# Weaving the first quarter of the output product into the last RWKV chain

## The reference, cut to what matters

```python
ya_l = chunk_gmlp(...)                  # 512 columns  = 4 tiles of 128
yb_l = rwkv_mixer(...)                  # 768 columns  = 6 tiles
yc_l = na_mixer(...)                    # 768 columns  = 6 tiles
mix_l = matmul(concatenate([ya_l, yb_l, yc_l]), w_out)       # (512 x 2048) @ (2048 x 2048)
xl = layer_norm(ALPHA * xl + g1 * mix_l, ln1_g, ln1_b)
xl = layer_norm(ALPHA * xl + g2 * sq_relu_mlp(xl * (1 + sc2) + sh2, w_up, w_down), ln2_g, ln2_b)
```

## Time and profile before

| | us |
|---|---|
| median of three runs | 3344.65 (3338.05 to 3346.8) |
| the profiled execution, its own time | 3334.03 |
| its span, first to last instruction | 3332.2 |
| mean granted clock | 0.959 of full speed |
| last small matmuls of pair 5 ahead of its chain end | 1625.3 |
| first matmul of the output product | 1687.9 |
| last matmul of the output product | 1863.6 |

### The profile page before, as it was taken

The page is one execution under the profiler, slowest core; times in us unless marked ns, Lnnn a source line. Parts: engine busy times, 40 slices in busy tenths (PEclk is TensorE's granted clock), DMA queues, the critical chain, the costliest instruction groups (busy, mean ns, idle before and its releaser), DMA issues.

```text
span 3332.2 us, 70508 instructions
## 1 busy us (share of the span) xinstructions
PE 3097.9 (93%) x30308; PEld 2582.9 (78%) x30308; DVE 1578.5 (47%) x1999; ACT 745.7 (22%) x1103; POOL 1057.0 (32%) x482
## 2 busy tenths in 40 slices
PE   6799997999995999999879899999999999999996
PEld 0677875787774999999768688888888888888885
DVE  0777768347865444555422644343333333333335
ACT  0322222012222222222122321212121222222221
POOL 0343333444330000000034344444444444444442
PEclk7799998999997999999889999999999999999998
DMA  9665657222423111110142122222222222222222
GB/s 406 232 221 199 211 197 246 79 71 105 153 87 151 50 45 51 53 53 14 42 189 100 63 96 94 100 91 98 94 94 94 94 94 94 94 96 97 96 96 107
DMA packets 97666, 387.40 MB, mean 116 GB/s; under 512 B 10912, under 2 KB 12704, under 8 KB 90912
## 3 DMA queue, kind: packets, MB, share of 16 engines
q1 hardware_dynamic: 72096, 289.45, 23.9%
q10 hardware_dynamic: 25056, 92.42, 7.8%
q0 software_dynamic: 288, 2.10, 0.2%
HBM read 352.73 MB, written 31.20 MB: 115 GB/s over the span
## 4 chain that ended last, share of the span: by engine, by line
PE 64%; DVE 3%; DMA 1%; issue 1%; ACT 0%; SPq 0%; POOL 0%; ACTq 0%; DVEq 0%; POOLq 0%
PE bank L884 16%; PE bank L885 16%; PE bank L886 16%; PE bank L632 12%; PE bank L648 1%; PE bank L708 1%; DMA buf<-small_lncol 1%; PE bank L696 1%; PE bank L776 0%; PE bank L774 0%; DVE buf L1781 0%; DVE buf L1782 0%; PE bank L656 0%; DVE buf L1492 0%; DVE buf L1737 0%
## 5 line engine op out<-in xcount | busy, mean ns | idle before, releaser
L498 POOL TENSOR_TENSOR buf<-buf 128x1024 fp32r<-128x1024 f32 x288 | 696.9, 2420 | 1610.4 <-ACT buf L1264 1610.4
L884 PE MATMUL bank<-buf 128*128 128x512 f32 x2304 | 903.6, 392 | 19.1 <-DVE buf L1702 18.5
L885 PE MATMUL bank<-buf 128*128 128x512 f32 x2304 | 903.2, 392 | 0.0
L886 PE MATMUL bank<-buf 128*128 128x512 f32 x2304 | 903.0, 392 | 0.0
L1264 ACT CAST buf<-buf 128x1024 fp32r<-128x1024 f32 x288 | 302.5, 1050 | 1252.9 <-PE bank L886 1251.9
L884 PEld LDWEIGHTS bank<-buf 128*128 128x128 f32 x2304 | 432.6, 188 | 117.4 <-issue 20.3
L886 PEld LDWEIGHTS bank<-buf 128*128 128x128 f32 x2304 | 432.6, 188 | 97.2
L885 PEld LDWEIGHTS bank<-buf 128*128 128x128 f32 x2304 | 432.6, 188 | 96.7
L632 PE MATMUL bank<-buf 64*64 64x64 f32 x13248 | 427.4, 220 | 22.8 <-issue 10.6
L522 PE MATMUL bank<-buf 128*128 128x512 f32 (+1 forms) x1168 | 430.1, 368 | 17.8 <-POOL buf L492 11.8
L632 PEld LDWEIGHTS bank<-buf 64*64 64x64 f32 x13248 | 411.6, 136 | 34.2 <-issue 30.2
(11 more groups left out here) (215 smaller groups left out, 2426.0 us busy)
## 6 DMA issues: line engine op xcount, KB each, us to landing
buf<-stream SPq DMA_DIRECT2D x382, 512.0 KB, 3.2
buf<-adarows ACTq DMA_DIRECT2D x108, 512.0 KB, 4.9
buf<-ada SPq DMA_DIRECT2D x32, 1024.0 KB, 12.9
scaled_keys<-buf ACTq DMA_DIRECT2D x18, 768.0 KB, 5.6
buf<-scaled_keys SPq DMA_DIRECT2D x18, 768.0 KB, 6.9
buf<-adarows SPq DMA_DIRECT2D x20, 512.0 KB, 6.3
buf<-tokens SPq DMA_DIRECT2D x4, 1536.0 KB, 21.9
buf<-bias ACTq DMA_DIRECT2D x6, 1024.0 KB, 5.2
```

The costliest lines, as they stand in the source:

```text
L498: G.tensor_tensor(wl2[b % SPLIT2], raw2[b], wh2[b % SPLIT2].bitcast(F32), ALU.subtract).then_inc(split2, 1)
L884: pe.matmul(bank[:, :], lh, rh, start=start, stop=False)
L885: pe.matmul(bank[:, :], lh, rl, start=False, stop=False)
L886: return pe.matmul(bank[:, :], ll, rh, start=False, stop=stop)
```

## The change

**Mixer tiles are split where they are made.** `gated` now multiplies in place, then casts into `late_h` and subtracts into `late_l`, both resident, so the RWKV tiles are no longer stored. Attention makes `mst` (high) and `mlow` (low), gMLP overwrites its buffers with high and low parts; both are stored as two DRAM tensors and loaded back as `early_h`, `early_l` (2 x 2.5 MB) during pair 5, ahead of the wait for its last products. The rows of the output weight are permuted on the host so that the ten early tiles come first.

**The product is woven in.** `mixer_product` is a generator of 32 groups of six matmuls per column block. Block n = 0 is advanced one group after each of the ten chain steps, two after `read`, four after `mean`, the rest after `variance`. Pieces 5, 6, 7 wait for `R["done"]` of 2, 4, 6. `normed(4)` moves behind chain step 1 and `gated(4)` behind step 3. ACT makes the high parts of pieces 0 to 7 inside `act_core`.

**Gate rows go through DRAM.** After gMLP, ACT stores the two gate columns to `gate_rows` element by element; they are read back as broadcasts. The 32 DVE copies, 32 PE products and 8 ACT copies go.

**Layout.** Buffers of the core and the second half are placed anew, so that pieces, early tiles and tokens can land while the core still runs.

```diff
+        def mixer_product(pe, n):
+            for c in range(KT // 2):
+                pos = 8 * n + c
+                pe.wait_ge(split2, pos + 1)
+                if n == 0 and c == 0:
+                    pe.wait_ge(mix_ld[0], 16)
+                    pe.wait_ge(mix_ld[1], 16)
+                if n == 0 and c >= 5:
+                    pe.wait_ge(R["done"], 2 * (c - 5) + 2)
+                for m in range(4):
+                    if c == 0 and n >= 2:
+                        pe.wait_ge(E["oev"], 4 * n + m + 1)
+                    for k in range(2):
+                        mm = triple(pe, banks[4 * (n % 2) + m], ...)
...
+                    yield
...
# pe_core
+            ready(pe, ("rc", BPAIRS - 1, 0), ("rc", BPAIRS - 1, 1))
+            groups = mixer_product(pe, 0)
             for n in range(1, NC - 1):
                 chain(BPAIRS - 1, n)
+                advance(groups, 1)
             read(BPAIRS - 1)
+            advance(groups, 2)
             mean(BPAIRS - 1)
+            advance(groups, 4)
             variance(BPAIRS - 1)
+            finish(groups)
...
# act_core, behind pair 5
+            for pos in range(4):
+                act_high_part(once, pos, 32, 0)
             read(BPAIRS - 1)
+            act_high_part(once, 4, 32, 0)
             square(BPAIRS - 1)
             deviation(BPAIRS - 1)
-            store(BPAIRS - 1)
+            for pos in range(5, 8):
+                act_high_part(once, pos, 32, 0)
...
# dve_core, gated
-                dve.wait_ge(mst_out, 16 * (1 + CPAIRS + j))
-                V.tensor_tensor(mst, yc, late[j % 2][:, SEQ:], ALU.mult).then_inc(R["done"], 1)
+                step(V.tensor_tensor(yc, yc, late[j % 2][:, SEQ:], ALU.mult))
+                step(V.tensor_copy(late_h[:, j, :], yc))
+                V.tensor_tensor(late_l[:, j, :], yc, late_h[:, j, :].bitcast(F32), ALU.subtract).then_inc(R["done"], 1)
...
             for n in range(1, NC - 1):
                 chain(BPAIRS - 1, n)
+                if n == 1:
+                    normed(BPAIRS - 2)
+                if n == 3:
+                    gated(BPAIRS - 2)
...
# SP
+            ready(sp, ("rc", last - 1, 1), ("gv", last, 2))
+            sp.dma_start(raw2[0], stream2[0]).then_inc(rawld2[0], 16)
...
+            sp.dma_start(early_h.bitcast(F32), mixhd.rearrange("k p t -> p k t")).then_inc(mix_ld[0], 16)
+            sp.dma_start(early_l.bitcast(F32), mixld.rearrange("k p t -> p k t")).then_inc(mix_ld[1], 16)
+            ready(sp, ("z", last, 2), ("w", last, 2))
+            for b in range(1, RING2):
                 sp.dma_start(raw2[b], stream2[b]).then_inc(rawld2[b], 16)
+            ready(sp, ("rc", last, 0), ("rc", last, 1), ("y", last - 1))
+            sp.wait_ge(R["done"], last)
+            sp.wait_ge(gates_out, 32)
             sp.dma_start(xr, xtok).then_inc(E["x"], 16)
+            sp.dma_start(grow1, gates[0:1].rearrange("o k p -> o (k p)").to_broadcast([P, D])).then_inc(E["grow"], 16)
...
# act_gmlp; act_second_half issues lncol, grow2, lng, lnb once R["done"] is 6
+            act.wait_ge(mod_ev, 6)
+            for c in range(2):
+                act.dma_start(gates[c].rearrange("k p -> p k"), modv[:, 2 + 3 * c, :, 0], allow_slow_non_contiguous=True).then_inc(gates_out, 16)
...
# dve_gmlp, per tile j (before: add, multiply)
+                V.tensor_tensor(gout[j], gout[j], gu[j], ALU.mult).then_inc(A["vch"], 1)
+                V.tensor_copy(gouth[j], gout[j]).then_inc(A["vch"], 1)
+                V.tensor_tensor(goutl[j], gout[j], gouth[j].bitcast(F32), ALU.subtract).then_inc(A["done"], 1)
```

More of the change, by code:

```diff
@@ L298, in build_block @@
         eye = masks[:, P * (4 + 2 * len(LEVELS)):]
[L299 to L308, removed]
+        fc(192)
+        AH, BH, KH = fc(NI * T), fc(NI * T), fc(NI * T)
+        BT, KTT, GT, cV, RH = [fc(NI * T)], [fc(NI * T)], fc(NI * T), fc(TOK), [fc(NL * T)]
+        fc(256)
+        VT, late, RB, RK = [fc(TOK)], [fc(2 * SEQ)], [fc(NL * T)], [fc(NL * T)]
+        BT.append(fc(NI * T))
+        KTT.append(fc(NI * T))
+        W = fc(NI * T)
+        RH.append(fc(NL * T))
+        AT, GV, TT, XT, X, LT = (fc(NI * T) for _ in range(6))
         VT.append(fc(TOK))
-        RH.append(fc(NL * T))
-        Z, W, TR, NK, M = (fc(NI * T) for _ in range(5))
         RB.append(fc(NL * T))
@@ L331, in build_block @@
         lncol, hscl, hshf = f2(2 * KT), f2(KT), f2(KT)
[L332 to L336, removed]
+        dtmp = [f2(512) for _ in range(2)]
+        hTl = f2(KT * SEQ, F32R).rearrange("p (k t) -> p k t", k=KT)
+        hidl = f2(FT * SEQ, F32R).rearrange("p (k t) -> p k t", k=FT)
         second.close()
@@ L354, in build_block @@
         xmod, xhigh, xsplit = sem("tokens_modulated"), sem("tokens_high_part"), sem("tokens_split")
-        mixraw_ld = [sem(f"mixer_outputs_loaded_{q}") for q in range(4)]
+        mix_ld = [sem(f"mixer_{part}_parts_loaded") for part in ("high", "low")]
+        gates_out = sem("gate_rows_stored")
         z_ev = sem("projections_copied")
@@ L888, in pe_second_half @@
         def pe_second_half(pe):
[L890 to L904, removed]
-                        t.wait(split2, 16, pos + 1)
-                        if n == 0:
-                            pe.wait_ge(E["mixl"], 2 * c + 2)
-                        for m in range(4):
-                            if c == 0:
-                                t.wait(E["oev"], 8, 4 * n + m + 1)
-                            for k in range(2):
-                                mm = triple(pe, banks[4 * n + m], mixh[:, 2 * c + k, P * m:P * m + P],
-                                            mixl[:, 2 * c + k, P * m:P * m + P], wh2[pos % 2][:, 512 * k:512 * k + 512],
-                                            wl2[pos % 2][:, 512 * k:512 * k + 512], c == 0 and k == 0, c == 7 and k == 1)
-                            if c == 7 and m < 3:
-                                mm.then_inc(E["omm"], 1)
-                        mm.then_inc(used2, 1)
+            for n in range(1, 4):
+                finish(mixer_product(pe, n))
             for k in range(KT):
@@ L1101, in act_projections, with act_high_part @@
                     squares(j + 1)
+        def act_high_part(t, pos, per, base):
+            t.wait(rawld2[pos % RING2], 16 * per // RING2, 16 * ((base + pos) // RING2) + 16)
+            if base + pos >= SPLIT2:
+                t.wait(used2, per, base + pos + 1 - SPLIT2)
+            nc.scalar.copy(wh2[pos % SPLIT2], raw2[pos % RING2]).then_inc(high2, 1)
         def act_core(act):
@@ L1635, in dve_attention @@
             w("pv", 8)
[L1636 to L1639 removed]
+            t.wait(mst_out, 32, 32)
+            rows = lambda a: a.rearrange("p (r b c) -> p b r c", b=4, c=QC)
+            outs = Q[4][:, :].rearrange("p (b r c) -> p b r c", b=4, c=QC)
+            t.step(V.tensor_copy(rows(mst), outs))
+            V.tensor_tensor(rows(mlow), outs, rows(mst.bitcast(F32)), ALU.subtract).then_inc(C["done"], 1)
             assert t.n == t.per, ("c", t.n)
@@ L1895 @@
     up, down = tiles(a["w_up"][0]), a["w_down"][0]
-    parts = [wide_tiles(a["w_out"][0])]
+    mixer = list(range(APAIRS)) + list(range(APAIRS + BPAIRS, KT)) + list(range(APAIRS, APAIRS + BPAIRS))
+    parts = [wide_tiles(a["w_out"][0].reshape(KT, P, D)[mixer].reshape(D, D))]
     for e in range(EFF):
```

141 lines of the change are left out of this document (64 added, 77 removed).

## The result

| | before | after |
|---|---|---|
| median of 4 runs, us | 3345.02 (3338.05 to 3346.8) | 3314.16 (3310.14 to 3319.46) |
| profiled execution, us | 3334.03 | 3313.88 |
| its span, us | 3332.2 | 3312.1 |

The ratio is 0.9921 with the 95% interval 0.9905 to 0.9938: 26 us faster by the ratio, 31 by the two medians, where 45 were forecast. Applied to 3344.65 the ratio gives 3318.2, which is just beyond the upper end of the range, 3318.

The account below looks back on a forecast made before the run. PE was taken as the bound, busy 93%, with 62.6 us between pair 5's small matmuls and the output product to fill. Gain 47.3 less 2.2 for earlier additions gave 45.1: 3299.5 us against the runs' median, range 3287 to 3318.

Parts of the forecast that it names:

- PE in the chain and the product: From pair 5's last small matmul to the output product's end: 1625.3 to 1816.6; gain 47.3 us.
- The narrow place, piece 4: Reload into piece 4's buffer during the weave: landed at 1651, needed by ACT at 1654; if late, some 5 us.
- The last mixer tile: After the variance at 1661.8, tile done at 1669.8; piece 7 wants it at 1678, 8 us of cover.
- The two stalls at steps 3 and 5: In the woven chain PE waits for DVE behind normed(4) and gated(4): 1.7 and 2.15 us, together 3.9.
- changes of shape: PE switches 22 times between 64 x 64 and 128 x 128 matmuls in the weave: 0.1 us each, 2.2 together.
- rival B: Weave too thin: stalls lower the clock or piece 4 comes late; gain 25 to 38, time 3307 to 3320; chance 0.22.
- sign that the prediction listed as wrong: PE waiting for POOL's low parts or last DVE subtraction, clock near 0.7, late ACT copies, or longer attention turns.
- Blocks 1 to 3 and all behind them run as before, shifted.: Output product after block 0, and everything later including the MLP: same duration as before, only earlier; no cost set.
- the early loads in pair 5 cost nothing: Loading early mixer tiles during pair 5: no term for slowing PE was set.
- What is added earlier: Extra work before the weave costs 2.2 us: gMLP 1.4, attention 0.75; core's longer gated and the gate store covered.
- The element-wise gate store: After gMLP, two stores of 2048 four-byte runs take ACT 10.6 us to issue, covered by idle time: cost 0.
- the prediction's slow case: Gate store decides from 0.25 us per run; at 0.31 PE waits 62 us, time 3361; chance 0.03.

Follow-up runs that it names:

- Runs 4 to 6: In order: changed kernel, small tiles moved behind MLP low parts, 3283.14 us; same move in kernel before, 3321.48; first one's operands shifted 8 to 320 words, 3282.29 to 3319.58.
- run 8: Changed kernel without the cast and subtraction that make low parts of the ten gMLP and attention tiles: 3309.83 us, ratio 0.9909.
- the kernel with the burst: Kernel before plus two useless DRAM-to-DRAM copies of 2.5 MB each at the time of the early loads: 3345.95 us, ratio 1.0025.

## Why the prediction fell short

**Right, by its own steps.** PE in the chain and the product: from the last small matmul of pair 5 to the product's end 190.8 us, by the prediction 191.3 (1625.3 to 1816.6). The 0.84 us ahead of the chain, which the view puts down to issue, stand where the prediction had 0.75 of waiting for the `rc` copies. Clock 1.00 through the read, 5.82 us for its 192 matmuls, 5.8 forecast. `lncol` is gone from the chain. The narrow place, piece 4, held: PE did not wait for POOL anywhere in the chain and the product. The last mixer tile: variance 1680.5, its last subtraction at 1691.06 on DVE, so done 11.2 us after the variance where 8.0 were forecast: 3.2 late against 8 us of cover. One of its operations, the cast, took 2.59 us and not 0.44, and ended right behind a subtraction of POOL (1688.35 to 1690.75): one blocking, of the kind that the prediction priced at up to 2.39, here on an operation with a single input. The Trainium skill (SBUF — State Buffer, Who interferes with whom) names casts among those that can take the shared port pair, and this row agrees.

**Right in sum only.** The two stalls at steps 3 and 5 are 0.67 and 0.94 us, not 1.7 and 2.15. A chain step without a stall is 1.96 us, from 1655.72 to 1657.68 in the timeline above, where the matmuls alone were set to 1.6. The 0.36 between them hold two changes of shape, so each costs about 0.18 where 0.1 was taken, 22 of them 4.0 us (an estimate: it puts the whole difference down to the changes). The two errors, 2.2 us too much and 1.8 too little, cancel, which is luck.

Luck too is where the time landed. 3314 us, or 3318 by the ratio, lies in what rival B names (3307 to 3320), but neither of B's causes came: the clock stayed at 1.00 and piece 4 was in time. And no sign that the prediction listed as wrong showed up in the changed part; only the last product matmul, at 1833.5 us instead of 1816 to 1820, told that the parts ahead of it had become longer, and the MLP had no sign at all.

**Wrong: "Blocks 1 to 3 and all behind them run as before, shifted."** The layout was in the diff, and it was costed at nothing, without naming what makes it so. The MLP takes 9.9 us more. Runs 4 to 6 show the cause: the addresses of the operands, and all distances tried fit a period of 64 words. The prediction had no case for it.

**Wrong: the early loads in pair 5 cost nothing.** The prediction used them as the reason why pieces come early and never asked what 5 MB at once do to PE. They cost 7.0 us in the stretch, and a burst alone costs 5.7. Behind the stretch 1.6 us more are lost, of which "issue" is 1.4. That is another case: SP's three raw pieces had landed at 1637.2 us, and the DMA engines were idle in the pause:

```profile
1637.70:1639.10 1.40, 0.02 (x2) 0.02 (x2) 0.62 (x1) 0.00 (x0) 0.48 (x1) 1.00 0.00 0
```

Every changed kernel has this pause, 0.6 to 1.7 us long, and no kernel before has it; what makes it stays open.

**Mis-sized: "What is added earlier", 2.2 us.** Of it 1.4 were for gMLP, in the stretch from the mix to the core. That stretch is 3.8 us longer in the two traces compared, and 2.6 on average over all kernels (run 8). The wait of PE's fourth mix came as forecast:

```profile
636.53 1.09 PE L923 MATMUL bank<-buf 128*64 128x128 f32 x16 [2.28 <-DVE buf L1691]
639.05 1.97 PE L923 MATMUL bank<-buf 128*64 128x128 f32 x16 [1.42 <-DVE buf L1691]
```

That wait was 0.23 us before, and PE is 1.6 us later behind it; the rest lies in the projections, is of the size of the scatter, and what makes it was not found. The 0.75 us for attention would stand ahead of the mix, where one code varies by 7 us between executions, so no trace can show them. The element-wise gate store was rightly set to nothing. In the timeline and in the row of its line (duration of the issues in ns, then the landing of the two in us):

```profile
646.72 1.98 ACTq L1288 DMA_DIRECT2D gate_rows<-buf  x2
659.94 0.86 ACT L1024 COPY buf<-bank 128x512 f32<-128x512 f32 x2 [33.42 <-PE bank L540]
...
L1288 ACTq DMA_DIRECT2D gate_rows<-buf x2: 472/975/1478, 646.7 to 647.2; - x2
...
DMA to landing us min/median/max: 14.5/17.5/20.5
```

ACT is free again at 648.7 and idle until 659.94. The store itself is not cheap: it lands in up to 20.5 us, where the whole tiles took 2.0. Its 4096 runs over 16 engines in about 20 us are 0.08 us each (estimated from this row), a third of the 0.25 at which the prediction's slow case began. That fits the sentence of the Trainium skill in the prediction (DMA: Bandwidth & Descriptors, Rules for kernel authors), one descriptor per element. The slow case also had ACT held by a full queue; the longer of the two issues is 1.48 us.

**The sum.** -47.7 + 9.9 + 7.0 + 1.6 + 3.8 + 0.4 = -25.0 us. The forecast mechanism was right, in place and in size; what failed was "all behind them run as before" (the MLP, 9.9 us) and the early loads taken as free (7.0 us): the assumption that the work around the change keeps its price.

## What to carry to other kernels

A diff that moves tiles in SBUF can change the price of every matmul that reads them: list each operand's start modulo 64 words before and after (as allocated, since a small tile may take more than its size), and keep the large operands of a matmul in step by putting small tiles last. Where a large transfer is moved under a part in which PE runs on many small matmuls, read "issue" in the waits of that part and, in the trace of before, wherever a transfer already runs under such work, and spread the transfer. Compare PE by the time for a fixed count of matmuls rather than by its busy share, since a slower rate looks like full use.

## What the runs showed of the hardware

Matmuls of 128 x 128 by 512 in this three-product form run at one per 0.2267 us (87.05 / 384) when all their SBUF operands lie 0, 64, 256 or 320 words past a multiple of 512 from one another, and at 0.231 to 0.2335 us (88.75 to 89.66) when some are 8, 16, 32 or 56 words off. Over 6144 of them that is 14 to 36 us. The Trainium skill (SBUF — State Buffer, Who interferes with whom) says that PE never waits for anyone at SBUF. That is about other engines, and these runs do not speak against it; but placement is not free for all that, since PE is slower here by its operands' addresses. Whether it is the distance between the operands or each one's own address that counts these runs cannot tell, since in all of them most operands stayed in place; nor do they tell what inside the memory makes it so.

With 5 MB in flight PE paused for up to 4.0 us with nothing to wait for that the profile shows, even when nothing was written to SBUF; the DMA engines moved 331 GB/s in that pause (1573.65 to 1577.66 of the kernel with the burst). The smaller loads under the same kind of work in the kernel before, DMA engines full too, go with pauses of 2.06 to 2.60 us. And a change between 64 x 64 and 128 x 128 matmuls costs PE about 0.18 us, an estimate from the 1.96 us of a woven chain step.
